# Two fused transformer blocks on one core: all modulation columns as row products on VectorE

## The chip, the cores and the metric

The kernel runs on one core of a Trainium2 chip. The metric is the device time of one execution in microseconds (us), lower is better. TensorE (PE) multiplies, VectorE (DVE) and ScalarE (ACT) work elementwise, GpSimd (POOL) and SyncE (SP) issue transfers here.

## The reference

Two blocks run one after the other on 256 tokens of width 1024, each with two layers. Every layer of both blocks is modulated: a conditioning vector goes through silu and is multiplied by a matrix, and the result, cut into columns of 1024, shifts, scales and gates the token stream.

```python
# first block, per layer l (6 columns of 1024 = 48 units of 128)
mod = silu(c) @ ada_w[l] + ada_b[l]
x = x + g1 * mixer(modulate(rms_norm(x), sh1, sc1))
x = x + g2 * peer_ffn(modulate(rms_norm(x), sh2, sc2), w_query, sub_keys, expert_u, expert_v)
# second block, per layer i (9 columns of 1024 = 72 units of 128)
m  = silu(c_2) @ ada_w_2[i] + ada_b_2[i]
mc = silu(c_ctx_2) @ ada_w_2[i] + ada_b_2[i]     # context: only layer 0, first 5 columns are read
```

`peer_ffn` picks 16 experts for each of 8 heads and token out of 128 x 128. The kernel computes all experts densely: a first phase (`expert_u`, 128 units) makes the activations of all experts, a second (`expert_v`, 128 units) sums them with gates.

## The kernel before, in words

**Stream.** All weights are one stream of units of 128 x 1024 float32 (512 KB). SP loads them in a written order into a ring of four slots, `raw`; the load of unit q waits until unit q-4 is released (`load`, line 496). A weight unit is split into a high and a low part: ACT copies each half to `wh` (`hi`, line 635, L643), DVE writes raw minus `wh` to `wl` (`lo`, line 1096, L1101), and PE makes three products of each 128 x 128 piece (L1906 to L1908), 24 matmuls in a unit. `wh` and `wl` hold two units.

**Stages.** `plan` (line 110) writes the order: for each layer of the first block `w_in`, `attn_o`, `w_out`, `query`, `sub_keys`, `expert_u`, `expert_v`; then the second block `ffn.0.0`, its context copy `ffn.0.0.x`, `kv_ctx`, `qkv`, `na_o`, `ffn.0.1`, `ffn.1.0`, `conv_in`, `conv_o`, `ffn.1.1`. DVE, ACT and PE each walk through that order by hand written code. In `w_out` DVE adds the product to the stream (L1157) and ACT squares it (L874). `pairs` (line 1161) runs the feed-forward stages in 22 rounds of three units, with hooks of vector work after chosen rounds.

**Modulation, two ways.** (1) *Folded on DVE.* `fold` (line 1106, L1119) multiplies a unit of the weights, laid out as columns, by the silu of the vector, which stands in every partition, and sums along the row: one column of 128 values. The unit takes a slot of the ring and is folded right behind `lo` of the unit before it. `folds_after` (line 73) says where: 16 at the start, 32 in layer 0 up to `query.0`, and 104 of the second block's in `ffn.0.0`, `ffn.0.0.x`, `kv_ctx`, `qkv`, `ffn.0.1` and `ffn.1.0`. (2) *On PE.* The 48 units of the first block's layer 1 (`ada1.1`) and 40 units of the second block's layer 0 (`ada2.0`, for both vectors) go through PE in the experts' first phase, after units with u % 5 in (0, 2), up to u = 119 in layer 0 and u = 99 in layer 1 (`MIXED_U`, line 58). `ada_unit` (line 2066, L2072) makes four matmuls with a moving block of 256; each eight units a block is copied by ACT (`copy_block`, line 790), turned by PE (`turn_block`, line 2056) and placed by ACT (`place_block`, line 796).

**The experts' first phase.** For u up to 59, DVE picks the experts (routing: maxima, replaced and found values over the scores), with `feed()` (line 1460), which is `lo` of the next unit, at chosen places between. From u = 60 (`GATES_FROM`) there is one batch of four tokens a unit: DVE makes two one-hot tiles (L1592, L1594), ACT weights one (L915), PE multiplies them (`spread_choices`, line 2193, L2200), ACT copies the result (L925). Each unit ends with ACT's gelu (L921) and POOL's store of it (L597). `add_bias` (line 1258) adds the bias to modulation columns before they are used.

Of the kernel before, what the change touches and what calls it, by code (L numbers as in the profile page):

```python
# [29 lines left out]
P = 128  # L30
# [26 lines left out]
MIXED_ADA = ("ada1.1", "ada2.0")  # L57
MIXED_U = (120, 100)
# [14 lines left out]
def folds_after():  # L73


    out = {}

    def put(stage, units, name, columns):
        assert len(units) == len(columns), (stage, len(units), len(columns))
        for k, column in zip(units, columns):  # L80
            out[stage, k] = (name, column)

    def rows_of(js):

# [7 lines left out]
    two = list(range(FOLDED_2))  # L92
# [9 lines left out]
FOLDED_2 = 72 - 40 + 72  # L102


def fold_column(n):

    return (0, 40 + n) if n < 32 else (1, n - 32)


def plan():  # L110
# [18 lines left out]
    for l in range(DEPTH):  # L129
# [7 lines left out]
        add(MIXED_ADA[l], 2 * MIXED_U[l] // 5, False)  # L137
# [15 lines left out]
    for name, units in (("fold1", 48), ("fold2", FOLDED_2)):  # L153
        fold_at[name] = placed
        placed += units

    order = [("fold1", k) for k in range(FIRST_FOLDS)]
    starts = {}
    for name, units, split, source, groups in rows:
        if name in MIXED_ADA:  # L160
            continue
        starts[name] = len(order)
        for k in range(units):
            order.append((name, k))
# [21 lines left out]
COLUMNS = [("c", KT), ("c_2", KT), ("c_ctx", KT), ("final_norm", KT)]  # L186
# [66 lines left out]
def build(nc, ctx, stream, columns, tables, x_in, ctx_in, rpb, c_rows, h_spill, out):  # L253
# [31 lines left out]
    c_first = side[:, 0:D].rearrange("p (n w) -> p n w", w=D // 2)  # L285
    c_second = side[:, :].rearrange("p (n w) -> p n w", w=6 * T)[:, :, 4 * T:6 * T]
# [13 lines left out]
    cs = sb("cs", [P, 3, KT])  # L300
    mod1 = sb("mod1", [P, DEPTH, 48])
    mod2 = sb("mod2", [P, DEPTH, 72, 2])
    mod2_flat = mod2[:, :, :, :].rearrange("p l n c -> p (l n c)")
# [5 lines left out]
    rows = sb("rows", [P, 2 * KT * P // 4])  # L309

    GROUPS, GROUP = 4, 32
    vectors = sb("vectors", [P, KT, GROUP])
    BLOCK = KT * P // GROUPS
# [55 lines left out]
    SUMS = 30720  # L369
    token_sums = tiles(SUMS, TT, D)  # L370
# [18 lines left out]
    silu_ready = sem("silu_ready")  # L389
    c_loaded = [sem(f"c_loaded{i}") for i in range(2)]  # L390
    c_ready = sem("c_ready")
    folded = sem("folded")
    block_copied = sem("block_copied")
    block_turned = sem("block_turned")
    block_placed = sem("block_placed")
# [67 lines left out]
    BLOCKS = [stages[name].units // KT for name in MIXED_ADA]  # L463

    def after(l, u):

        return [2 * (u // 5) + u % 5 // 2] if u < MIXED_U[l] and u % 5 in (0, 2) else []
# [17 lines left out]
    def _(sp):  # L485
        seen = Seen()

        def released(q):

            name, k = order[q]  # L490
            if name in fold_at:
                return folded, folded_units.index((name, k)) + 1
# [11 lines left out]
        sp.dma_start(c_first, c_rows[0, :, :].rearrange("p (n w) -> p n w", w=D // 2)).then_inc(c_loaded[0], 16)  # L504
# [30 lines left out]
        for st in stages.values():  # L535

            if st.name in MIXED_ADA:
                continue
            if st.name.startswith("expert_u") or st.name in mixed_stages:
# [35 lines left out]
    def _(pool):  # L575

        pool.dma_start(X[:, :, :], x_in).then_inc(x_loaded, 16)
# [6 lines left out]
        pool.memset(vectors[:, :, :], 0.0).then_inc(constants_set, 1)  # L584
        pool.wait_ge(constants_set, 4)
# [20 lines left out]
        pool.dma_start(c_second, c_rows[1, :, :].rearrange("p (n w) -> p n w", w=D // 2)).then_inc(c_loaded[1], 16)  # L606
# [23 lines left out]
    def _(act):  # L630
# [143 lines left out]
        def silu_of_rows(view, n):  # L774

            act.wait_ge(c_loaded[n], 16)
            act.activation(view, view, ACT.Silu).then_inc(c_ready, 1)

        silu_of_rows(c_first, 0)
        act.wait_ge(prepared, 48)  # L780
        act.wait_ge(constants_set, 5)
        for k, name in enumerate(("c", "c_2", "c_ctx")):
            last = act.activation(cs[:, k, :], column(name, 0, KT), ACT.Silu)
        last.then_inc(act_step, steps.one())
        act.wait_ge(act_step, steps.n)
        act.activation(vectors[:, :, 0], cs[:, 1, :], ACT.Copy)
        act.activation(vectors[:, :, 1], cs[:, 2, :], ACT.Copy)
        act.activation(vectors[:, :, 2], cs[:, 0, :], ACT.Copy).then_inc(silu_ready, 1)

        def copy_block(n, used):  # L790

            act.wait_ge(raw_used, used)
            act.activation(rows[:, (n % 2) * BLOCK:(n % 2 + 1) * BLOCK], banks[6 + n % 2][:, 0:BLOCK],
                           ACT.Copy).then_inc(block_copied, 1)

        def place_block(n, nv, dst):

            row = 0 if nv == 2 else 2
            act.wait_ge(block_turned, n + 1)
            turned = banks[2 + n % 2][:, 0:2 * P].rearrange("p (f g r) -> p g f r", f=2, g=GROUPS)  # L800
            act.activation(dst.rearrange("p (g f v) -> p g f v", f=2, v=nv), turned[:, :, :, row:row + nv],
                           ACT.Copy).then_inc(block_placed, 1)

        def block_home(n):

            if n < 6:
                return 1, mod1[:, 1, KT * n:KT * (n + 1)]
            return 2, mod2_flat[:, 2 * KT * (n - 6):2 * KT * (n - 5)]
# [4 lines left out]
        for l in range(DEPTH):  # L813
# [87 lines left out]
            first, first_block = l * BATCHES, BLOCKS[0] * l  # L901
            used = stages[MIXED_ADA[l]].r
            for u in range(KEYS):
# [5 lines left out]
                b = u - GATES_FROM  # L909
                if 0 <= b < BATCHES:  # L910
# [11 lines left out]
                b = u - GATES_FROM - 2  # L922
# [1620 lines left out]
```

## Time and profile before

| | us |
|---|---|
| median of 3 runs | 3757.21 |
| lowest and highest | 3756.78, 3763.63 |
| the profiled execution, its own time | 3760.27 |
| its span in the trace | 3758.1 |
| PE busy | 3591.4 (96%) |
| DVE busy | 2690.9 (72%) |
| ACT busy | 2034.6 (54%) |
| bytes moved | 784.65 MB, mean 209 GB/s |

Busy shares are averages over stages. A PE matmul's end is modelled, so the pace of units, read from one ACT instruction to the same one of the next unit, says more than the share. "Released by" in a wait names what came last by the profile.

### The profile page before, as it was taken

What the parts mean: (1) busy time and instruction counts of PE and PEld (TensorE: products, weight loads), DVE (VectorE), ACT (ScalarE), POOL (GpSimd) and SP (SyncE); (2) the same over time, 40 slices, a digit from 0 to 9 for tenths busy, and PEclk for the clock granted to TensorE, in tenths of its full rate; (3) what the DMA queues carried; (4) which work ended last, traced back from release to release, by engine and by line L of the source; (5) the groups of instructions that cost most, each with busy time, mean ns of one, the idle gap of its engine ahead of it and who ended that gap; (6) DMA issues with size and microseconds to landing.
All of it is one profiled execution on the core that took longest, in us unless ns stands there. A gap on an engine that the chain in (4) does not pass through costs nothing.

```text
span 3758.1 us, 71030 instructions
## 1 busy us (share of the span) xinstructions
PE 3591.4 (96%) x24950; PEld 3281.8 (87%) x24950; DVE 2690.9 (72%) x5336; ACT 2034.6 (54%) x4235; POOL 217.2 (6%) x335
## 2 busy tenths in 40 slices
PE   5989999999999989999999998999998899999898
PEld 5889999998888889999998887899987689898898
DVE  6774986667777664896667777777777577776765
ACT  4544447775555554447775555544444454545444
POOL 0000111110000000111110001010001010100000
PEclk8999999999999999999999999999999999999999
DMA  8456776667775434776647778776765167575453
GB/s 281 154 187 213 269 269 213 213 220 240 242 241 190 137 129 168 249 264 230 214 170 254 242 240 252 229 246 214 245 219 168 32 201 248 197 247 167 140 185 133
DMA packets 245507, 784.65 MB, mean 209 GB/s; under 512 B 30048, under 2 KB 62816, under 8 KB 245040
## 3 DMA queue, kind: packets, MB, share of 16 engines
q1 hardware_dynamic: 230544, 737.78, 59.5%
q0 software_dynamic: 14752, 44.12, 3.3%
q8 instruction: 125, 2.05, 0.2%
q14 instruction: 86, 0.70, 0.1%
HBM read 747.17 MB, written 34.60 MB: 208 GB/s over the span
## 4 chain that ended last, share of the span: by engine, by line
PE 77%; DVE 7%; PEld 6%; issue 3%; DMA 3%; ACT 2%; PEldq 1%; SPq 0%; ACTq 0%; POOL 0%; DVEq 0%
PE bank L1906 17%; PE bank L1907 17%; PE bank L1908 17%; PE bank L1979 5%; PE bank L1980 5%; PE bank L1981 5%; PE bank L2200 3%; PEld bank L1979 2%; PEld bank L1980 2%; PEld bank L1981 2%; DVE wl L1101 2%; DMA raw<-stream 2%; PE bank L2050 2%; PE bank L2072 1%; ACT wh L643 1%
## 5 line engine op out<-in xcount | busy, mean ns | idle before, releaser
L1101 DVE TENSOR_TENSOR wl<-raw,wh 128x512 fp32r<-128x512 f32 x2180 | 1453.8, 690 | 687.2 <-ACT wh L643 684.8
L643 ACT ACTIVATE wh<-raw 128x512 fp32r<-128x512 f32 x2180 | 1316.5, 629 | 825.3 <-PE bank L1981 427.0
L1906 PE MATMUL bank<-XH,wh 128*128 128x256 f32 x5184 | 1504.0, 290 | 88.0 <-DVE XL L1226 49.9
L1907 PE MATMUL bank<-XL,wh 128*128 128x256 f32 x5184 | 1477.4, 285 | 0.0
L1908 PE MATMUL bank<-XH,wl 128*128 128x256 f32 x5184 | 1476.6, 285 | 0.0
L1906 PEld LDWEIGHTS bank<-XH,wh 128*128 128x128 f32 x5184 | 1004.4, 194 | 129.6 <-issue 92.0
L1907 PEld LDWEIGHTS bank<-XL,wh 128*128 128x128 f32 x5184 | 1005.9, 194 | 4.0 <-issue 1.0
L1908 PEld LDWEIGHTS bank<-XH,wl 128*128 128x128 f32 x5184 | 1004.7, 194 | 0.0
L1979 PE MATMUL bank<-wh,AH 128*128 128x512 f32 x1464 | 571.4, 390 | 1.4 <-DVE AL L1609 1.0
L1980 PE MATMUL bank<-wl,AH 128*128 128x512 f32 x1464 | 570.8, 390 | 0.0
L1981 PE MATMUL bank<-wh,AL 128*128 128x512 f32 x1464 | 569.6, 389 | 0.0
L1981 PEld LDWEIGHTS bank<-wh,AL 128*128 128x128 f32 x1464 | 274.9, 188 | 58.0
L1979 PEld LDWEIGHTS bank<-wh,AH 128*128 128x128 f32 x1464 | 275.3, 188 | 57.3 <-DVE wl L1101 1.7
L1980 PEld LDWEIGHTS bank<-wl,AH 128*128 128x128 f32 x1464 | 275.3, 188 | 52.8
L921 ACT ACTIVATE side<-bank 128x256 f32<-128x256 f32 x256 | 98.3, 384 | 323.6 <-PE bank L1908 319.6
L686 ACT ACTIVATE arena<-bank 128x256 f32<-128x256 f32 (+1 forms) x208 | 79.2, 383 | 319.4 <-PE bank L1908 319.3
L597 POOL DMA_DIRECT2D h_spill<-side x256 | 138.4, 541 | 1491.1 <-ACT side L921 1478.5
L1594 DVE TENSOR_TENSOR side<-iota,routed 128x512 f32<-128x512 f32 x128 | 88.7, 693 | 152.9 <-PE bank L2200 152.9
L1119 DVE SCALAR_TENSOR_TENSOR raw<-raw,side 128x1024 f32<-128x1024 f32 x152 | 186.2, 1225 | 15.0 <-DMA raw<-stream 14.8
L1906 PE MATMUL bank<-X2H,wh 128*128 128x256 f32 x544 | 157.0, 289 | 6.2 <-DVE wl L1101 5.9
L915 ACT ACTIVATE side<-side,routed 128x128 f32<-128x128 f32 x512 | 162.9, 397 | 0.0
L1601 DVE TENSOR_TENSOR side<-side,arena 128x256 f32<-128x256 f32 x256 | 159.5, 623 | 0.1
(237 smaller groups left out, 3146.4 us busy)
## 6 DMA issues: line engine op xcount, KB each, us to landing
raw<-stream SPq DMA_DIRECT2D x1340, 512.0 KB, 4.3
h_spill<-side POOLq DMA_DIRECT2D x256, 128.0 KB, 3.7
side<-h_spill SPq DMA_DIRECT2D x256, 128.0 KB, 3.8
arena<-rpb POOLq DMA_DIRECT2D x4, 1024.0 KB, 25.3
arena<-tables POOLq DMA_DIRECT2D x2, 832.0 KB, 9.5
X<-x_t POOLq DMA_DIRECT2D x1, 1024.0 KB, 8.2
side<-ctx_t POOLq DMA_DIRECT2D x8, 128.0 KB, 3.9
arena<-ctx_t POOLq DMA_DIRECT2D x1, 1024.0 KB, 8.3
```

Source lines behind the costliest of these rows:

```text
L597: pool.dma_start(h_spill[u, :, :], HS[:, u % 2, :]).then_inc(h_stored[u % 2], 16)
L643: act.activation(wh[:, n % 4, :], raw[:, q % 4, HALF * half:HALF * (half + 1)], ACT.Copy).then_inc(hi_ready, 1)
L915: last = act.activation(by_weight[:, b % 2, n * P:(n + 1) * P], unweighted[:, n * P:(n + 1) * P], ACT.Copy, scale=routed[:, 2, t:t + 1])
L1101: tt_op(wl[:, n % 4, :], raw[:, q % 4, HALF * half:HALF * (half + 1)], wh[:, n % 4, :].bitcast(F32), SUB).then_inc(lo_ready, 1)
L1119: dve.scalar_tensor_tensor(unit, unit, 1.0, c, MUL, MUL, accum_out=dst).then_inc(folded, 1)
L1601: tt_op(AP_[:, j % 2, :].unsqueeze(2), HV[:, j % 4, :].unsqueeze(2), gates[:, :, bass.ds(j + more, 1)], MUL).then_inc(gate_done, 1)
L1906: pe.matmul(out, wh[:, n % 4, a:b], moving_h, start=start, stop=False, skip_group_check=check)
L1907: pe.matmul(out, wh[:, n % 4, a:b], moving_l, start=False, stop=False, skip_group_check=check)
L1908: return pe.matmul(out, wl[:, n % 4, a:b], moving_h, start=False, stop=stop, skip_group_check=check)
L1979: pe.matmul(out, high, wh[:, n % 4, :], start=first, stop=False)
L1980: pe.matmul(out, high, wl[:, n % 4, :], start=False, stop=False)
L1981: last = pe.matmul(out, low, wh[:, n % 4, :], start=False, stop=final)
```

## The change

The PE way is taken out, with its copies, turns and placements on ACT and PE and the small ACT work that made the vectors for it. All 48 + 48 + 144 units are folded on DVE; the 40 units of the second block's layer 0 that the context reads too are folded twice, once with each vector (280 folded products, 152 before). The number of units streamed, 240, is the same. Where they go:

```diff
-    put("w_in.0", (2, 3, 4, 6, 7, 8, 10, 11, 12, 14, 16, 18, 20, 22, 24, 26), "fold1", one[16:32])
-    put("attn_o.0", (1, 3, 5, 7), "fold1", one[32:36])
-    put("w_out.0", (1, 2, 4, 5), "fold1", one[36:40])
-    put("query.0", range(2, 32, 4), "fold1", one[40:48])
...
-    put("ffn.0.0", rows_of(range(2, 21)), "fold2", two[0:19])
-    put("ffn.0.0.x", rows_of(range(21)), "fold2", two[19:40])
-    put("kv_ctx", (0, 1, 2, 3, 5, 7, 9, 11, 13, 15), "fold2", two[40:50])
-    put("qkv", range(1, 24, 2), "fold2", two[50:62])
-    put("ffn.0.1", rows_of(range(21)), "fold2", two[62:83])
-    put("ffn.1.0", rows_of(range(21)), "fold2", two[83:104])
+    def beside_layer(l, name, columns):
+
+        put(f"w_in.{l}", (2, 3, 4, 6, 7, 8, 10, 11, 12, 14, 16, 18, 20, 22, 24, 26), name, columns[0:16])
+        put(f"attn_o.{l}", (1, 3, 5, 7), name, columns[16:20])
+        put(f"w_out.{l}", (1, 2, 4, 5), name, columns[20:24])
+        put(f"query.{l}", range(2, 32, 4), name, columns[24:32])
...
+    beside_layer(0, "fold1.0", one[16:48])
+    put("expert_u.0", range(66, 114, 3), "fold1.1", one[0:16])
+    beside_layer(1, "fold1.1", one[16:48])
+    two = list(range(DEPTH * 72))
+    put("query.1", range(0, 32, 4), "fold2", two[40:48])
+    put("expert_u.1", range(66, 114, 3), "fold2", two[0:16])
+    put("ffn.0.0", rows_of(range(2, 21)), "fold2", two[16:35])
+    put("ffn.0.0.x", rows_of(range(21)), "fold2", two[35:40] + two[48:64])
+    put("kv_ctx", (0, 1, 2, 3, 5, 7, 9, 11, 13, 15), "fold2", two[64:74])
+    put("qkv", (0, 1, 2, 3, 5, 7, 9, 11, 13, 15, 17, 19, 21, 23), "fold2", two[74:88])
+    put("ffn.0.1", rows_of(range(21)), "fold2", two[88:109])
+    put("ffn.1.0", rows_of(range(21)), "fold2", two[109:130])
+    put("conv_in", range(1, 13, 2), "fold2", two[130:136])
+    put("ffn.1.1", rows_of(range(8)), "fold2", two[136:144])
```

The fold itself, with the second product ahead of the first where n < 40:

```diff
             unit = raw[:, q % 4, :].rearrange("p (n w) -> p n w", w=D // 2)
+            if name == "fold2" and n < 40:
+                dve.wait_ge(context_c_loaded, 16)
+                dve.scalar_tensor_tensor(unread, unit, 1.0, c_kept[:, :, :], MUL, MUL,
+                                         accum_out=second_mod(0, n, n + 1, 1))
             dve.scalar_tensor_tensor(unit, unit, 1.0, c, MUL, MUL, accum_out=dst).then_inc(folded, 1)
```

The silu of all three vectors' rows is made at the start: the first vector's stays in SBUF (`c_kept`), the other two (1 MB together) are loaded at the head of POOL's queue, go through ACT, and are stored to a DRAM scratch. They come back in 512 KB loads on POOL's queue: two copies of the second vector's once the operands of `w_in.1` are made, ahead of layer 1's table load, which used to be issued as soon as layer 0's second phase ended; the context vector's into `c_kept` after layer 1's last column; and one in the place where the rows of `c_2` were loaded before.

```diff
+        for n in range(2):
+            pool.dma_start(c_rows_at[:, n * D:(n + 1) * D], c_rows[1 + n, :, :]).then_inc(rows_loaded, 16)
         pool.dma_start(X[:, :, :], x_in).then_inc(x_loaded, 16)
...
             if l:
+                pool.wait_ge(xl_ready, made["w_in.1"])
+                pool.dma_start(c_query, c_spill[0, :, :].rearrange("p (n w) -> p n w", w=D // 2))\
+                    .then_inc(query_c_loaded, 16)
+                pool.dma_start(c_experts, c_spill[0, :, :].rearrange("p (n w) -> p n w", w=D // 2))\
+                    .then_inc(experts_c_loaded, 16)
                 pool.wait_ge(space_free, l)
...
+            if l == 0:
+                pool.wait_ge(c_ready, 2)
+                for n in range(2):
+                    pool.dma_start(c_spill[n, :, :], c_rows_at[:, n * D:(n + 1) * D]).then_inc(c_stored, 16)
+                pool.wait_ge(c_stored, 32)
+            else:
+                pool.wait_ge(folded, folds_by("fold1.1", 47))
+                pool.dma_start(c_kept[:, :, :], c_spill[1, :, :].rearrange("p (n w) -> p n w", w=D // 2))\
+                    .then_inc(context_c_loaded, 16)
```

The batches of the gates keep their pace, one a unit from u = 60 on. `add_bias` waits for the last column it needs and runs in smaller pieces (layer 1 of the first block as layer 0; the second block's just ahead of each use). Stages that hold folds are written out on SP, ACT and DVE where they were loops.

## Rows read from the trace of the kernel before

**Rows 1.** the page, part 1: busy us, share of the span, instructions

```profile
PE 3591.4 (96%) x24950; PEld 3281.8 (87%) x24950; DVE 2690.9 (72%) x5336; ACT 2034.6 (54%) x4235; POOL 217.2 (6%) x335
```

**Rows 2.** windows: us, then PE, PEld, DVE, ACT, POOL busy, clock, DMA share, GB/s

```profile
371.00:556.00 185.00, 183.40 (x1558) 169.64 (x1557) 171.43 (x524) 88.92 (x181) 30.81 (x57) 1.00 0.78 270
1891.00:1973.00 82.00, 82.00 (x699) 82.00 (x698) 53.16 (x83) 64.39 (x167) 11.35 (x21) 1.00 0.49 167
```

**Rows 3.** source line L2072, the modulation products on PE

```profile
L2072 PE MATMUL bank<-raw,vectors x704: 379/391/404, 371.0 to 1866.2; 128*32 128x256 f32 x176
```

**Rows 4.** timeline, ACT, layer 0 routing: start us, us, engine, line

```profile
429.42 0.38 ACT L921 ACTIVATE side<-bank 128x256 f32<-128x256 f32 x1 [2.21 <-PE bank L1908]
...
432.30 0.38 ACT L921 ACTIVATE side<-bank 128x256 f32<-128x256 f32 x1 [1.18 <-PE bank L1908]
```

**Rows 5.** timeline, ACT, layer 0 gates

```profile
646.79 0.38 ACT L921 ACTIVATE side<-bank 128x256 f32<-128x256 f32 x1 [0.69 <-PE bank L1908]
...
651.49 0.38 ACT L921 ACTIVATE side<-bank 128x256 f32<-128x256 f32 x1 [1.53 <-PE bank L1908]
...
655.25 0.38 ACT L921 ACTIVATE side<-bank 128x256 f32<-128x256 f32 x1 [0.50 <-PE bank L1908]
...
659.78 0.38 ACT L921 ACTIVATE side<-bank 128x256 f32<-128x256 f32 x1 [1.39 <-PE bank L1908]
```

**Rows 6.** timeline, DVE, layer 1 gates

```profile
1902.40 1.29 DVE L1101 TENSOR_TENSOR wl<-raw,wh 128x512 fp32r<-128x512 f32 x2
1904.00 0.69 DVE L1592 TENSOR_TENSOR side<-iota,routed 128x512 f32<-128x512 f32 x1 [0.31 <-ACT side L915]
```

**Rows 7.** timeline, ACT, layer 1 gates

```profile
1906.46 1.27 ACT L915 ACTIVATE side<-side,routed 128x128 f32<-128x128 f32 x4
1908.43 0.38 ACT L921 ACTIVATE side<-bank 128x256 f32<-128x256 f32 x1 [0.70 <-PE bank L1908]
```

**Rows 8.** the page, part 5: the folded products

```profile
L1119 DVE SCALAR_TENSOR_TENSOR raw<-raw,side 128x1024 f32<-128x1024 f32 x152 | 186.2, 1225 | 15.0 <-DMA raw<-stream 14.8
```

**Rows 9.** chain that ended last, in order of time: start us, us, what

```profile
38.76 1.68 DVE arena L1248
...
214.42 2.20 DVE arena L1429
...
250.79 3.47 PE bank L2050 x16
...
353.65 14.56 PE bank L2183 x128
...
1192.20 1.76 DVE arena L1248
...
1366.66 2.20 DVE arena L1429
...
1399.02 3.47 PE bank L2050 x16
...
1502.97 14.56 PE bank L2183 x128
...
2554.99 2.65 DVE arena L1675 x8
```

**Rows 10.** windows of the start

```profile
5.00:10.00 5.00, 0.00 (x0) 0.00 (x0) 1.49 (x3) 0.46 (x1) 0.00 (x0) 1.00 1.01 417
30.00:38.00 8.00, 0.00 (x0) 0.00 (x0) 6.04 (x12) 2.30 (x4) 0.00 (x0) 0.50 0.94 312
```

**Rows 11.** timeline, DVE, ffn.0.0, rounds 6 and 11

```profile
2415.90 0.41 DVE L1685 TENSOR_TENSOR side<-side,bank 128x256 f32<-128x256 f32 x1
...
2425.10 0.41 DVE L1685 TENSOR_TENSOR side<-side,bank 128x256 f32<-128x256 f32 x1
...
2460.24 0.41 DVE L1685 TENSOR_TENSOR side<-side,bank 128x256 f32<-128x256 f32 x1
...
2468.74 0.41 DVE L1685 TENSOR_TENSOR side<-side,bank 128x256 f32<-128x256 f32 x1
```

More of the change, by code:

```diff
@@ L152, in plan @@
     fold_at = {}
-    for name, units in (("fold1", 48), ("fold2", FOLDED_2)):
+    for name, units in (("fold1.0", 48), ("fold1.1", 48), ("fold2", 72 * DEPTH)):
         fold_at[name] = placed
         placed += units
-    order = [("fold1", k) for k in range(FIRST_FOLDS)]
+    order = [("fold1.0", k) for k in range(FIRST_FOLDS)]
     starts = {}
     for name, units, split, source, groups in rows:
-        if name in MIXED_ADA:
-            continue
         starts[name] = len(order)
@@ L307, in build @@
     routed = sb("routed", [P, 3, T])
[L309 to L313, printed above, removed]
+    c_kept = sb("c_kept", [P, 2, D // 2])
     small = sb("small", [P, 64])
@@ L369, in build @@
     SUMS = 30720
+    c_experts = tiles(SUMS + D, 2, D // 2)
+    unread_experts, unread_ffn = tiles(SUMS, 2, D // 2), tiles(QT, 2, D // 2)
     token_sums = tiles(SUMS, TT, D)
@@ L388, in build @@
     constants_set = sem("constants_set")
[L389 to L390 removed]
+    c_loaded = sem("c_loaded")
+    rows_loaded = sem("rows_loaded")
+    c_stored = sem("c_stored")
+    query_c_loaded = sem("query_c_loaded")
+    experts_c_loaded = sem("experts_c_loaded")
+    context_c_loaded = sem("context_c_loaded")
+    ffn_c_loaded = sem("ffn_c_loaded")
     c_ready = sem("c_ready")
     folded = sem("folded")
[L393 to L395 removed]
     mod_ready = sem("mod_ready")
@@ L460, in build, with folds_by, batches_of @@
     block = ctx.enter_context(nc.Block())
-    BLOCKS = [stages[name].units // KT for name in MIXED_ADA]
-    def after(l, u):
-        return [2 * (u // 5) + u % 5 // 2] if u < MIXED_U[l] and u % 5 in (0, 2) else []
+    def folds_by(name, k):
+        return folded_units.index((name, k)) + 1
+    def batches_of(u):
+        return [b for b in range(BATCHES) if GATES_FROM + b == u]
     CTX_FROM = 103
@@ L772, in copy_sum @@
                                ACT.Copy).then_inc(sum_copied[0], 1)
[L774 to L779, printed above, removed]
+        act.wait_ge(c_loaded, 16)
+        act.activation(c_kept[:, :, :], c_kept[:, :, :], ACT.Silu).then_inc(c_ready, 1)
+        act.wait_ge(rows_loaded, 32)
+        act.activation(c_rows_at, c_rows_at, ACT.Silu).then_inc(c_ready, 1)
         act.wait_ge(prepared, 48)
[L781 to L808, printed above, removed]
+        act.wait_ge(constants_set, 4)
         rms = A(RMS, T)
@@ L899, in row_highs @@
                 act.activation(AH[:, j % 2, :], AP_[:, j % 2, :], ACT.Copy).then_inc(row_high, 1)
-            first, first_block = l * BATCHES, BLOCKS[0] * l
-            used = stages[MIXED_ADA[l]].r
+            first = l * BATCHES
             for u in range(KEYS):
@@ L1266, in add_bias @@
             else:
-                bias = column(f"ada_b_2.{l}", a, b - a)
-                view = mod2[:, l, a:b, 0:sides]
-                step(tt_op(view, view, bias.unsqueeze(2).broadcast_to([P, b - a, sides]), ADD))
+                for side in range(sides):
+                    view = second_mod(l, a, b, side)
+                    step(tt_op(view, view, column(f"ada_b_2.{l}", a, b - a), ADD))
             settle()
@@ L1317, in _ @@
                 for n in range(FIRST_FOLDS):
-                    fold("fold1", n)
+                    fold("start", "fold1.0", n)
                 dve.wait_ge(prepared, 48)
-                add_bias(0, 1, 0, 16, units=FIRST_FOLDS)
+                add_bias(0, 1, 0, 16)
                 scale_plus_one(scale[:, :], mod1[:, l, 8:16], column(f"norm_mix.{l}", 0, KT))
@@ L1458, in _ @@
             fed = [1]
+            dve.wait_ge(c_stored, 32)
             def feed():
@@ L1588, in _ @@
             for b in range(BATCHES):
-                feed()
+                while fed[0] <= GATES_FROM + b:
+                    feed()
                 if b or l:
@@ L1811, in _ @@
         dve.wait_ge(view_ready, 1 + 2 * KT)
-        add_bias(0, 2, 40, 72, units=48 + 32)
+        add_bias(0, 2, 40, 48)
+        add_bias(0, 2, 48, 72)
         residual_factor(0, 24, 0, 1.0)
@@ L2208, in _ @@
                     pe.wait_ge(route_evacuated, 8 * (l + 1))
-                for a in after(l, u):
-                    ada_unit(first_block + a // KT, a % KT, place[MIXED_ADA[l], a])
-                n = block_after(l, u, 3)
-                if n is not None:
-                    turn_block(first_block + n)
                 if u == TURN_AT:
```

169 lines of the change are left out of this document (59 added, 110 removed).

## The prediction

> **What bounds the kernel now.** I read the busy shares first [rows 1]: PE is busy 96% of the span, DVE 72%. An average over stages says little, so the windows come next. The change takes its work off PE in one place only, the experts' first phase, so that is where any gain must come from. It has two parts with different limits. In the routing part of layer 0 (units 0 to 57) PE is busy 183.4 of 185 us, but DVE is busy 171.4 of the same 185 [rows 2]: PE leads by little, and DVE idles only 13.6 us. In the gates part (from unit 60) PE is busy all of 82 us, DVE 53.2 and ACT 64.4 [rows 2]. There PE bounds alone.
>
> Then the work to be removed [rows 3]: 704 matmul records, 8 for each of 88 units. Their own durations overlap and say nothing of their price; the pace of units does. ACT's gelu of one unit to that of the next is 2.88 us in the routing part where no modulation unit stands between [rows 4]. In the gates part it is 3.76 us without one, 4.53 with one, and 4.70 with one and the turn of a block [rows 5]. So a modulation unit costs 0.77 us of PE, a block's turn 0.17.
>
> **Gates part.** It holds 24 of layer 0's 48 modulation units and 16 of layer 1's 40: 40 x 0.77 = 30.8, and 7 turns x 0.17 = 1.2, together 32.0 us, all on the path. What comes instead is 16 folds in layer 0 and 16 double folds in layer 1, one every third unit, on DVE. A fold is one instruction of 1.225 us [rows 8], and its accumulator read hides in the pitch. After `lo` DVE is free at 1903.69; it makes the one-hot at 1904.00 to 1904.69, and ACT takes it up only at 1906.46 [rows 6, 7]: 1.77 us of slack. A double fold of 2.45 brings that one-hot to 1906.83, 0.4 late; ACT's weighting would be late by that, but ACT then waits 0.70 for PE before the gelu [rows 7], which takes it in. A single fold is not late at all. I take 0 for both; if the cover is gone, the next thing late is the gelu, then PE's bank. Bounds: 0 and 16 x 1.225 + 16 x 2.45 = 58.8.
>
> **Routing part.** 24 units x 0.77 and 2 turns x 0.17, 18.8 us of PE, go in each layer, and nothing is added. DVE's work stays, 171.4 of 185, so 13.6 is the most that can come back. It can't all come: where DVE has little to do between two `feed()` PE's 2.88 stays the limit, and DVE idles still. I take half, 7 us a layer, 14 in both; bounds 0 and 27.
>
> **Start.** DVE's 16 folds wait for their loads. The transfers run at 417 GB/s early and 312 late with the engines' share near 1 [rows 10]: the start is bound by transfers. The change adds 1.05 MB of reads at the head of POOL's queue, ahead of X, and 1.05 MB of writes. 2.1 MB take 5.0 us at 417 and 6.7 at 312. Some hides behind DVE, which catches up a little (its folds are 16 x 1.225 = 19.6 of the 38.8 us up to the reciprocal, [rows 9]): I take 4.5, bounds 0 and 6.7. ACT's larger silu and the removed small ones lie in its idle time.
>
> The page "DMA: Bandwidth & Descriptors" of the Trainium skill, section Specifications, gives a core about 358 GB/s of HBM as its limit; the row of 417 GB/s is above it, so the row decides here. By the page's figure the 2.1 MB would be an estimated 5.9 us and the sum 1.4 us higher.
>
> **Layer 1 from `w_in.1` to `query.1`.** It gets the 32 folds that layer 0 has, at the same units, and layer 0 against layer 1 in the trace is that experiment. From the reciprocal to `sub_keys`: 353.65 - 38.76 = 314.9 in layer 0, 1502.97 - 1192.20 = 310.8 in layer 1, a difference of 4.1. Nearly all is in `w_out`: 36.4 (214.42 to 250.79) against 32.4 (1366.66 to 1399.02) [rows 9]. There each fold stands between `lo` and DVE's residual, for which ACT's square and then ACT's next copy wait, so 4 folds cost about 1 us each; elsewhere DVE has idle time. So +4.1. The 8 further folds of `query.1` I take at 0 by the same comparison (its 8 folds of layer 0 did not show), bounds 0 and 9.8. The bias additions become more and smaller: +0.5.
>
> **POOL's queue in layer 1.** The table load is now issued behind the wait for the operands of `w_in.1` and behind two loads of 512 KB, while the ring runs 1.5 units a product unit. Together 1.9 MB, 4.5 us of all transfer engines at 417 GB/s. The ring is four units ahead, and the tables are needed only after 12 units of 2.88, 35 us: I take +1.5, bounds 0 and 4.5. The context vector's load stands ahead of the first store of layer 1 and lands during `sub_keys`: 0.
>
> **ffn.0.0 and after.** 19 folds become double. A plain round takes 8.50 us and is PE's; a round with operand work hooked on takes 9.20 [rows 11], because DVE and ACT hand tiles to one another there. In that chain a fold is exposed in full. Five rounds (5 to 9) have it: 5 x 1.225 = 6.1; the rest hides. In `ffn.0.0.x` five more, of which one stands right ahead of centring the context, which is on the chain (at 2554.99) [rows 9], 1.2, and 0.4 for two more bias additions. In `qkv` two more folds beside the bias mask's additions, worth at most 2.4: I take 1.0. The folds of `conv_in` and `ffn.1.1` are 0: plain rounds have room. Bounds for all this: 2 and 20.
>
> **Sum.** Gains 32.0 + 14 = 46.0. Costs 4.5 + 4.1 + 0.5 + 1.5 + 6.1 + 1.6 + 1.0 = 19.3. Net 26.7 us off the profiled execution's own 3760.3: 3733.6. The median of the three runs is 3.1 lower, so the forecast is 3757.2 - 26.7 = 3730.5, say 3731.
>
> **Rivals.**
> (A) *The routing part gives nothing, and the transfers cost their upper bounds.* DVE's 171 of 185 us and hand-written places of `feed()` speak for it, PE's 99% busy against. +14 + 2.2 + 3.0: 3750.
> (B) *DVE's room in routing is used in full and the start hides its bytes.* For it, POOL's loads are early; against, the start's full transfer engines. -13 - 4.5: 3713.
> (C) *Slower: the gates' folds are exposed.* Place: the chain one-hot, weighting, `spread_choices`, where a double fold is 0.4 over the slack of 1.77 and only ACT's 0.70 covers it. If the batches can't catch up within three units, each fold is paid: up to 58.8, 3790. It decides from 46% of that, 27 us; below, the change still gains. Against it: DVE is idle 28.8 of 82 us there [rows 2], 1.3 us in each unit of 3.76.
> (D) *Double folds in `ffn.0.0` are exposed in most rounds, not five.* 14 more rounds x 1.225 = 17: 3748.
> That the modulation doesn't leave PE can't be: L2072 is gone from the code.
>
> **How the numbers follow.** Forecast 0.58, A 0.12, B 0.12, C 0.05, D 0.13. The range 3713 to 3751 holds all but C and the outer ends. A measurement of this kernel tells about 0.2%, 7.5 us, from no change: same is 3749.7 to 3764.7. The forecast, B, and most of D and half of A are below: faster 0.87. Same 0.08, slower 0.05.
>
> **What would show it.** In the profile after: no L2072; gelu to gelu 3.76 through the gates of both layers, also at units with a fold; routing near 178 us to unit 57, with DVE hardly idle; the first reciprocal (L1248) near 43 us in place of 38.76; `w_out` of layer 1 as long as layer 0's 36.4; rounds 5 to 9 of `ffn.0.0` near 10.4 us. Rounds of the gates above 3.9 us would mean C; a start or a `w_in.1` longer by over 7 us would mean that transfers cost more than I took.

## The result, and the profile after

The changed kernel takes 3729.35 us (median of 4 runs, 3724.82 to 3734.11), the kernel before beside it on the same chip 3760.42 (3756.78 to 3764.11): a ratio of 0.9916, 95% interval 0.9902 to 0.9930. The forecast was 3731 us, in a range of 3713 to 3751. Measured again, five times, it took 3730.32 against 3758.65, ratio 0.9921 (0.9908 to 0.9935). The profiled execution of the changed kernel, 3734.11 by its own time with a span of 3732.3, is the slowest of its four, so what follows explains 26.2 us (3760.27 - 3734.11); the medians say 31.1 and, the second time, 28.3.

The page, parts 1 and 5, against [rows 1, 8]; L1092 is the last product of a fold, L1090 the product with the context vector:

```profile
PE 3533.5 (95%) x24224; PEld 3265.2 (87%) x24224; DVE 2830.1 (76%) x5602; ACT 2021.7 (54%) x4202; POOL 227.7 (6%) x341
...
L1092 DVE SCALAR_TENSOR_TENSOR raw<-raw,side 128x1024 f32<-128x1024 f32 x128 | 156.8, 1225 | 0.2 <-DMA raw<-stream 0.2
```

PE lost 57.9 us of busy time, and the span 25.8: more than half of what PE was relieved of didn't reach the end. DVE gained 139.2. (A bracket in the rows below holds the engine's idle time before the instruction, and what ended it.) The windows, against [rows 2], first the whole routing part of layer 0 (units 0 to 57), then 82 us of layer 1's gates with folds in them:

```profile
375.00:552.00 177.00, 169.30 (x1371) 165.49 (x1371) 170.59 (x524) 86.87 (x177) 30.81 (x57) 1.00 0.69 215
1860.00:1942.00 82.00, 81.92 (x690) 81.55 (x689) 57.27 (x96) 63.02 (x161) 11.89 (x22) 1.00 0.61 198
```

Routing: PE is no longer full, it idles 7.7 of 177 us, and DVE idles 6.4 (13.6 of 185 before). Gates: PE is as full as before. The timeline there, ACT, with the gelu (L897), the weighting (L891) and the copy of the gates (L902), against [rows 5, 7]:

```profile
1874.61 0.38 ACT L897 ACTIVATE side<-bank 128x256 f32<-128x256 f32 x1 [0.69 <-PE bank L1884]
...
1878.38 0.38 ACT L897 ACTIVATE side<-bank 128x256 f32<-128x256 f32 x1 [0.70 <-PE bank L1884]
...
1880.33 1.28 ACT L891 ACTIVATE side<-side,routed 128x128 f32<-128x128 f32 x4
1882.15 0.38 ACT L897 ACTIVATE side<-bank 128x256 f32<-128x256 f32 x1 [0.53 <-PE bank L1884]
```

and DVE in the same stretch, against [rows 6]:

```profile
1876.12 1.28 DVE L1068 TENSOR_TENSOR wl<-raw,wh 128x512 fp32r<-128x512 f32 x2
1877.32 1.22 DVE L1090 SCALAR_TENSOR_TENSOR arena<-raw,c_kept 128x1024 f32<-128x1024 f32 x1
...
1878.46 1.22 DVE L1092 SCALAR_TENSOR_TENSOR raw<-raw,arena 128x1024 f32<-128x1024 f32 x1
...
1879.61 0.69 DVE L1563 TENSOR_TENSOR side<-iota,routed 128x512 f32<-128x512 f32 x1
1880.82 1.28 DVE L1068 TENSOR_TENSOR wl<-raw,wh 128x512 fp32r<-128x512 f32 x2
1883.65 1.28 DVE L1068 TENSOR_TENSOR wl<-raw,wh 128x512 fp32r<-128x512 f32 x2
1887.42 1.28 DVE L1068 TENSOR_TENSOR wl<-raw,wh 128x512 fp32r<-128x512 f32 x2
```

Gelu to gelu is 3.77 us on both sides of a double fold. The one-hot behind it starts at 1879.61, 1.9 us later than one pace behind the one before (1873.95); ACT's weighting is 0.15 late, and the gelu not at all. Last the chain in order of time, against [rows 9]. Two rows have the source lines 1221 (the first reciprocal of a norm) and 1400 (the start of `w_out`); `bank L2026` is the mean of the squares that ends a stage; `ACT arena L803` comes late in `w_in` (the last units of the stage stand behind it):

```profile
42.51 1.67 DVE arena L1221
...
218.56 2.20 DVE arena L1400
...
254.94 3.47 PE bank L2026 x16
...
1168.37 1.76 DVE arena L1221
1180.32 7.45 DMA raw<-stream
1214.11 2.34 ACT arena L803
...
1347.03 2.20 DVE arena L1400
...
1383.42 3.47 PE bank L2026 x16
...
2348.42 3.46 PE bank L2026 x16
...
2515.67 3.46 PE bank L2026 x16
```

Stage by stage, both from their profiled executions (the same instruction to the same instruction; layer 0, layer 1):

| stretch | before | after | difference |
|---|---|---|---|
| up to the first reciprocal | 38.8 | 42.5 | +3.8 |
| `w_in` of layer 1, from the reciprocal to the row of L803 | 41.8 | 45.7 | +3.9 |
| `w_out` | 36.4, 32.4 | 36.4, 36.4 | 0, +4.0 |
| routing, gelu of unit 0 to 57 | 185.0, 185.4 | 176.8, 176.8 | -8.2, -8.6 |
| gelu of unit 57 to 60 | 10.0, 10.0 | 9.3, 9.3 | -0.7, -0.7 |
| gates, gelu of unit 60 to 127 | 269.3, 263.3 | 250.2, 250.6 | -19.1, -12.7 |
| `expert_v.1` and up to `ffn.0.0` | 405.4 | 406.7 | +1.3 |
| `ffn.0.0` | 161.4 | 167.3 | +5.8 |
| `ffn.0.0.x` | 203.3 | 204.7 | +1.4 |
| `kv_ctx` to the end of `na_o` | 241.6 | 244.9 | +3.3 |
| the four stages after it | 729.0 | 728.8 | -0.1 |

### The profile page after: what moved, and what is told of

The parts are those of the page before. It is cut to its first block, busy times and chain, and to the rows that moved or that the text cites. A ratio compares the mean times of both kernels' runs of the same rounds, so it can differ in the third digit from the quotient of the medians.

```text
span 3732.3 us, 68910 instructions
## 1 busy us (share of the span) xinstructions
PE 3533.5 (95%) x24224; PEld 3265.2 (87%) x24224; DVE 2830.1 (76%) x5602; ACT 2021.7 (54%) x4202; POOL 227.7 (6%) x341
## 4 chain that ended last, share of the span: by engine, by line
PE 69%; DVE 15%; PEld 7%; issue 3%; ACT 3%; DMA 2%; PEldq 1%; SPq 0%; ACTq 0%; DVEq 0%; POOL 0%
PE bank L1882 15%; PE bank L1884 15%; PE bank L1883 15%; PE bank L1955 5%; PE bank L1956 5%; PE bank L1957 5%; DVE wl L1068 5%; PE bank L2154 3%; PEld bank L1957 2%; PEld bank L1955 2%; PEld bank L1956 2%; DMA raw<-stream 2%; PE bank L2026 2%; ACT wh L650 1%; DVE raw L1092 1%
## 5 line engine op out<-in xcount | busy, mean ns | idle before, releaser
L1957 PEld LDWEIGHTS bank<-wh,AL 128*128 128x128 f32 x1464 | 275.0, 188 | 57.9
L693 ACT ACTIVATE arena<-bank 128x256 f32<-128x256 f32 x208 | 79.0, 382 | 327.6 <-PE bank L1884 327.3
L897 ACT ACTIVATE side<-bank 128x256 f32<-128x256 f32 x256 | 98.1, 383 | 288.1 <-PE bank L1884 284.3
L891 ACT ACTIVATE side<-side,routed 128x128 f32<-128x128 f32 x512 | 162.8, 396 | 0.7
L1092 DVE SCALAR_TENSOR_TENSOR raw<-raw,side 128x1024 f32<-128x1024 f32 x128 | 156.8, 1225 | 0.2 <-DMA raw<-stream 0.2
L1884 PE MATMUL bank<-X2H,wl 128*128 128x256 f32 x544 | 155.4, 286 | 0.0
```

Of the source, the lines that this page charges most:

```text
L891: last = act.activation(by_weight[:, b % 2, n * P:(n + 1) * P], unweighted[:, n * P:(n + 1) * P], ACT.Copy, scale=routed[:, 2, t:t + 1])
L1092: dve.scalar_tensor_tensor(unit, unit, 1.0, c, MUL, MUL, accum_out=dst).then_inc(folded, 1)
L1884: return pe.matmul(out, wl[:, n % 4, a:b], moving_h, start=False, stop=stop, skip_group_check=check)
L1957: last = pe.matmul(out, low, wh[:, n % 4, :], start=False, stop=final)
```

## The experiments

Each is the changed kernel with one edit, or, where it says so, the kernel before. Experiments 1 to 9 have one time each; the kernel before took 3763.33 beside 1 to 4, and 3765.26 beside 5 to 8. Experiments 1 to 4 ran on one chip, 5 to 8 on another, 9 and 10 on a third. Times of stretches are from their traces, against the table above. One stretch differs from trace to trace even where no edit touches it: up to the first reciprocal the changed kernel takes 42.5 us in its first trace, and 42.8 to 43.6 in the seven others that leave the start as it is. So a stretch is compared with those of the same chip where the difference is small.

**1. The rows of the two vectors later.** Their loads, silu and stores move from the head of the queues to behind `w_in.0`; ACT makes the silu in four pieces between products.

```diff
-        for n in range(2):
-            pool.dma_start(c_rows_at[:, n * D:(n + 1) * D], c_rows[1 + n, :, :]).then_inc(rows_loaded, 16)
...
             if l == 0:
-                pool.wait_ge(c_ready, 2)
+                pool.wait_ge(group_free, 2 + stages["w_in.0"].g + W_IN_TILES)
+                for n in range(2):
+                    pool.dma_start(c_rows_at[:, n * D:(n + 1) * D], c_rows[1 + n, :, :]).then_inc(rows_loaded, 16)
+                pool.wait_ge(c_ready, 5)
```

> The rows of the two vectors are loaded, put through silu (in four pieces, on ACT between units of attn_o.0) and spilled after w_in.0, not at the start. Theory (the start is bound by transfers, and 2.1 MB more of them cost 3.75 us): the first reciprocal of DVE comes back from 42.51 us to 38.8 (within 0.7), attn_o.0 grows by 0 to 1.5 us, the span falls by 2 to 4 us. Rival (the first reciprocal is late because DVE's folds or the new semaphores are slower): it stays near 42.5.

**2. The same bytes, other order.** The two loads only go behind those of X, the columns and the first tables on POOL's queue.

```diff
-        for n in range(2):
-            pool.dma_start(c_rows_at[:, n * D:(n + 1) * D], c_rows[1 + n, :, :]).then_inc(rows_loaded, 16)
         pool.dma_start(X[:, :, :], x_in).then_inc(x_loaded, 16)
...
         pool.dma_start(iota[:, :], tables[:, tab_at["iota"][0]:tab_at["iota"][0] + P]).then_inc(prepared, 16)
+        for n in range(2):
+            pool.dma_start(c_rows_at[:, n * D:(n + 1) * D], c_rows[1 + n, :, :]).then_inc(rows_loaded, 16)
```

> Only the order on POOL's queue is changed: X, the columns and the small tables first, the two row loads behind them. Theory (bytes, whatever their order): the first reciprocal stays at 42.5 us within 1 us. Rival (order: X and the columns come late, so the squares, the root and the bias are late): it comes back to 39 to 40 us.

Measured: 3728.38 and 3728.52 us. The reciprocal, in the chains of the first and the second:

```profile
38.38 1.67 DVE arena L1235
```

```profile
41.96 1.68 DVE arena L1221
```

Moving the bytes away gives 4.1 us of the start back (42.51 to 38.38), moving them behind X only 0.55. Against experiments 3 and 4, on the same chip, whose first reciprocals start at 43.38 and 43.30, it is about 5 and 1.4. So it is mostly the bytes that the start pays for; the place of X in the queue may be a quarter of it. The first pays 0.6 back in the stretch behind `w_in.0`, up to `w_out` (126.3 from 125.7).

**3. Layer 1's loads later.** The tables are loaded first, as in the kernel before; the two copies of the second vector's silu come after `w_in.1`.

```diff
             if l:
-                pool.wait_ge(xl_ready, made["w_in.1"])
-                pool.dma_start(c_query, c_spill[0, :, :].rearrange("p (n w) -> p n w", w=D // 2))\
-                    .then_inc(query_c_loaded, 16)
-                pool.dma_start(c_experts, c_spill[0, :, :].rearrange("p (n w) -> p n w", w=D // 2))\
-                    .then_inc(experts_c_loaded, 16)
                 pool.wait_ge(space_free, l)
...
             else:
+                pool.wait_ge(group_free, 2 + stages["w_in.1"].g + W_IN_TILES)
+                pool.dma_start(c_query, c_spill[0, :, :].rearrange("p (n w) -> p n w", w=D // 2))\
+                    .then_inc(query_c_loaded, 16)
+                pool.dma_start(c_experts, c_spill[0, :, :].rearrange("p (n w) -> p n w", w=D // 2))\
+                    .then_inc(experts_c_loaded, 16)
                 pool.wait_ge(folded, folds_by("fold1.1", 47))
```

> Layer 1's table load is issued at the end of layer 0's second phase again, and the two copies of the second vector are loaded only after w_in.1, while attention runs. Theory (the 1.9 MB beside a ring at 1.75 units a product unit starve the first units of w_in.1): from the reciprocal to the head sums 52.95 us falls to the 50.3 of layer 0, which has the same folds; the span falls by 2.5 us. Rival (the folds themselves cost it): it stays at 52.9.

Measured: 3730.23 us; `w_in.1` falls from 45.7 to 41.6 (1168.32 to 1209.94, chain), by more than I expected. Windows of the same 20 us, 12 us behind a reciprocal that starts at 1168.3 to 1168.4 in both, of the changed kernel and of this one; then POOL's issues in the changed kernel:

```profile
1180.00:1200.00 20.00, 16.78 (x127) 16.57 (x128) 12.39 (x21) 7.53 (x17) 0.00 (x0) 0.91 0.85 307
```

```profile
1180.00:1200.00 20.00, 19.47 (x162) 19.26 (x162) 14.98 (x26) 9.62 (x20) 0.00 (x0) 1.00 0.85 298
```

```profile
1177.42 0.54 POOL L585 DMA_DIRECT2D side<-c_spill  x1 [364.58 <-DVE XL L1199]
1177.95 0.54 POOL L587 DMA_DIRECT2D arena<-c_spill  x1
1178.48 0.53 POOL L590 DMA_DIRECT2D arena<-tables  x1
```

The three loads, 1.9 MB, share the transfer engines with the ring just when DVE folds three units in four. Without them PE has 162 matmul records in the 20 us, with them 127, and idles 3.2 us, and its granted clock falls to a mean of 0.91. The transfer engines' share is 0.85 in both: they aren't short of time in the mean, the ring's loads come late (one stands for 7.45 us in the chain above, and for 5.29 in this one). `w_in.1` has its 16 folds in both kernels of this comparison: the loads cost all of its 4 us, the folds nothing. The time as a whole moved by less than single runs differ, so the verdict rests on the stretch.

**4. A third product in every double fold of `expert_u.1`**, to find how much cover the gates have.

```diff
                 dve.scalar_tensor_tensor(unread, unit, 1.0, c_kept[:, :, :], MUL, MUL,
                                          accum_out=second_mod(0, n, n + 1, 1))
+                if host == "expert_u.1":
+                    dve.scalar_tensor_tensor(tiles(SUMS - D, 2, D // 2), unit, 1.0, c_kept[:, :, :], MUL, MUL,
+                                             accum_out=small[:, 63:64])
```

> In the gates part of layer 1 each double fold has a third product beside it (its result is not used), 16 x 1.225 = 19.6 us of DVE work more. Theory (the cover is 1.77 us of slack at the one-hot plus 0.70 us of ACT's wait for PE, 2.47 in all, and a double fold of 2.45 just fits): three products of 3.68 are 1.2 us over it, so units with a fold take up to 4.9 us in place of 3.77, 10 to 19 us in all. Rival (DVE runs ahead and the cover spans several units, 28.8 of 82 us idle): the pace stays 3.77 and the span within 2 us.

Measured: 3732.9 us; gates of layer 1 250.7 us, from 250.6. My expectation was wrong; the rival is right on the sum. DVE around the same unit as above, and ACT's weighting in it:

```profile
1875.95 1.28 DVE L1068 TENSOR_TENSOR wl<-raw,wh 128x512 fp32r<-128x512 f32 x2
...
1881.31 1.28 ACT L891 ACTIVATE side<-side,routed 128x128 f32<-128x128 f32 x4 [1.19 <-DVE side L1566]
...
1881.80 1.28 DVE L1068 TENSOR_TENSOR wl<-raw,wh 128x512 fp32r<-128x512 f32 x2
1884.21 1.28 DVE L1068 TENSOR_TENSOR wl<-raw,wh 128x512 fp32r<-128x512 f32 x2
1887.27 1.28 DVE L1068 TENSOR_TENSOR wl<-raw,wh 128x512 fp32r<-128x512 f32 x2
1891.04 1.28 DVE L1068 TENSOR_TENSOR wl<-raw,wh 128x512 fp32r<-128x512 f32 x2
```

`lo` starts 5.85, 2.41, 3.06 and 3.77 us apart; with two products it was 4.70, 2.83 and 3.77. DVE is late by 2.1 and makes it good over the next two units, because it needn't wait there. The lateness does get as far as ACT: its weighting waits 1.19 us for DVE, and the gelu of each such unit comes after 4.28 us, the next one after 3.27. PE doesn't feel it: it is busy 81.91 of 82 us (1860 to 1942), as with two products. So 3.67 us of products in one place cost nothing in the sum, though the waits of a single unit, 1.77 and 0.70, don't add up to that.

**5. `qkv` with 12 folds as before**, two moved to `kv_ctx`.

```diff
-    put("kv_ctx", (0, 1, 2, 3, 5, 7, 9, 11, 13, 15), "fold2", two[64:74])
-    put("qkv", (0, 1, 2, 3, 5, 7, 9, 11, 13, 15, 17, 19, 21, 23), "fold2", two[74:88])
+    put("kv_ctx", (0, 1, 2, 3, 4, 5, 6, 7, 9, 11, 13, 15), "fold2", two[64:76])
+    put("qkv", range(1, 24, 2), "fold2", two[76:88])
```

> qkv has its 12 folds of before again (after units 1, 3, 5, ...), and the two others go to kv_ctx, after units 4 and 6. Theory (folds beside the bias mask's additions in the first units of qkv are exposed, and those in kv_ctx's idle time are not): from the mean of kv_ctx (2720.2 us) to that after na_o (2985.5 us), 265.3 us, comes back to 262 to 263; the span falls by 2 to 3 us. Rival (the longer stage comes from the many small bias additions, or is chance): it stays at 265.

Measured: 3732.1 us, `kv_ctx` to `na_o` 244.3, from 244.9 (and from 245.1 in the three others on the same chip). My theory fell: the two folds are worth 0.8 at most of the 3.3. The same stretch in the second profile of the unaltered changed kernel is 242.6, and between 242.7 and 245.1 in the eight other variants; the kernel before has 241.6, and 240.1 in the variant of experiment 9. In the first profile the chain has a wait for the ring here that most of the others lack:

```profile
2771.05 5.70 DMA raw<-stream
```

The stretch is longer by 3.3 in the first two profiles (244.9 against 241.6), and by 2.5 in two that ran on one chip (242.6 against 240.1): about 2.5 to 3.3 us of it are real. What causes them stays open. It is hardly the ring alone: ACT's copies wait 6.5 us for loads there in the first profile and not at all in the kernel before, but in this experiment they wait only 0.2, and the stretch is 244.3.

**6. No folds in rounds 5 to 9 of `ffn.0.0`.** 20 double folds stand in `expert_u.1` in place of 16, one more in `kv_ctx`.

```diff
-    put("expert_u.1", range(66, 114, 3), "fold2", two[0:16])
-    put("ffn.0.0", rows_of(range(2, 21)), "fold2", two[16:35])
+    put("expert_u.1", range(62, 122, 3), "fold2", two[0:20])
+    put("ffn.0.0", rows_of([2, 3, 4] + list(range(10, 21))), "fold2", two[20:34])
```

> Rounds 5 to 9 of ffn.0.0 hold no fold; four more double folds stand in expert_u.1 (20, after every third unit from 62) and one fold more in kv_ctx. Theory (in these rounds DVE and ACT hand tiles to one another and a double fold is exposed twice 1.225): rounds of 9.5 to 10.26 us fall to 8.5, or to 8.7 where hooked work remains, so ffn.0.0 is shorter by 6 to 8 us, and expert_u.1 keeps its pace of 3.77. Rival (the hooked work alone makes the rounds long): they stay over 9 us, and the stage falls by under 3 us.

Measured: 3723.31 us. `ffn.0.0` takes 158.9, from 167.3, a little more than I expected, and the gates of layer 1 keep their 250.6. DVE's product that ends a round (L1656) in the changed kernel, against [rows 11], and in this one:

```profile
2402.32 0.41 DVE L1656 TENSOR_TENSOR side<-side,bank 128x256 f32<-128x256 f32 x1
...
2412.58 0.41 DVE L1656 TENSOR_TENSOR side<-side,bank 128x256 f32<-128x256 f32 x1
...
2420.99 0.41 DVE L1656 TENSOR_TENSOR side<-side,bank 128x256 f32<-128x256 f32 x1
```

```profile
2390.87 0.41 DVE L1656 TENSOR_TENSOR side<-side,bank 128x256 f32<-128x256 f32 x1
2399.37 0.41 DVE L1656 TENSOR_TENSOR side<-side,bank 128x256 f32<-128x256 f32 x1
```

Rounds of 10.26 become 8.50. So the fold was exposed there, as predicted, and one fold had cost even the kernel before: 158.9 is 2.5 below its 161.4. The 9.20 of [rows 11] was not the operand work's alone, as the prediction has it: with that work and no fold a round takes 8.50. `ffn.0.0.x` pays 1.1 back.

**7. `w_out` without folds**, its four moved into `w_in`, which then has 20, the last four behind units 28 to 31.

```diff
-        put(f"w_in.{l}", (2, 3, 4, 6, 7, 8, 10, 11, 12, 14, 16, 18, 20, 22, 24, 26), name, columns[0:16])
-        put(f"attn_o.{l}", (1, 3, 5, 7), name, columns[16:20])
-        put(f"w_out.{l}", (1, 2, 4, 5), name, columns[20:24])
+        put(f"w_in.{l}", (2, 3, 5, 6, 8, 9, 11, 12, 14, 15, 16, 18, 20, 22, 24, 26, 28, 29, 30, 31), name, columns[0:20])
+        put(f"attn_o.{l}", (1, 3, 5, 7), name, columns[20:24])
```

> The four folds of w_out in both layers go to w_in, which has 20 in place of 16, spaced wider at its start and to its last unit. Theory (in w_out a fold lies on the chain lo, residual, square, copy; in w_in it is covered): w_out falls from 36.3 us to 32.4 in both layers, w_in keeps its length within 1 us in each, the span falls by 7 to 8 us. Rival (the transfers of w_in can't carry more): w_in grows by 2 us or more in each layer and takes back half of it or more.

Measured: 3730.51 us. `w_out` is 32.4 in both layers (1348.41 to 1380.84 in layer 1's chain), 3.9 less, and `w_in` up to the row of L803 is no longer. But the stretch from 7 us behind that row to `w_out` is 127.5 and 127.7, from 125.7. The first 50 us behind the row are as before; then, where the chain of the changed kernel is PE's alone, that of this one waits for two loads of the ring, around the folds of units 28 to 31:

```profile
1275.56 5.00 DMA raw<-stream
...
1283.71 4.87 DMA raw<-stream
```

So half of the gain comes back, as the rival said, only later than it said; by this chain it is loads of the ring that come late where four units in a row have a fold behind them. The term of `w_out` is confirmed, the new place was badly chosen.

**8. Less of DVE in routing.** The second of the two key look-ups is left out: the column index is a copy of the row index. So 13.7 us of DVE's instructions a layer are left out.

```diff
                 for side, top, dst in ((0, TOPA, RI), (1, TOPB, RJ)):
+                    if side:
+                        feed()
+                        feed()
+                        settle()
+                        step(dve.tensor_copy(A(RJ, P), A(RI, P)))
+                        feed()
+                        continue
```

> The kernel after the change, with one of the two look-ups of the routing (compare, multiply and sum of 2048 elements, 3 x 2.28 us, for each half of the tokens) left out and the other's result copied, so the second key index is not computed; 13.7 us of DVE work less in each layer. Theory (DVE bounds the routing part now, at 167 of 170 us busy, except where PE's 2.88 us does): the 176.8 us to unit 57 fall by 4 to 9 us in each layer. Rival (PE or the waits between engines bound it): under 1.5 us.

Measured: 3728.96 us, routing 174.8 in each layer, from 176.8. The window of layer 0's routing:

```profile
375.00:552.00 177.00, 170.32 (x1394) 167.73 (x1393) 159.21 (x523) 87.65 (x179) 31.35 (x58) 1.00 0.69 218
```

and the gelus of the changed kernel, then of this one, at the place of the look-up:

```profile
445.54 0.38 ACT L897 ACTIVATE side<-bank 128x256 f32<-128x256 f32 x1 [1.74 <-PE bank L1884]
448.92 0.38 ACT L897 ACTIVATE side<-bank 128x256 f32<-128x256 f32 x1 [1.96 <-PE bank L1884]
452.34 0.38 ACT L897 ACTIVATE side<-bank 128x256 f32<-128x256 f32 x1 [2.00 <-PE bank L1884]
```

```profile
444.64 0.38 ACT L897 ACTIVATE side<-bank 128x256 f32<-128x256 f32 x1 [1.74 <-PE bank L1891]
448.04 0.38 ACT L897 ACTIVATE side<-bank 128x256 f32<-128x256 f32 x1 [1.98 <-PE bank L1891]
450.92 0.38 ACT L897 ACTIVATE side<-bank 128x256 f32<-128x256 f32 x1 [1.46 <-PE bank L1891]
```

Of 13.7 us less work, 2.0 reach the pace, between theory and rival: the rounds of the look-up fall from 3.42 and 3.41 to PE's 2.88, and the other long rounds (3.29, 3.62, 3.52, 4.24, 4.36) stay. DVE now idles 17.8 of 177 us, and the time is as good as the same. DVE's total doesn't set routing; in the look-up's rounds it is the work between two `feed()`. Not all long rounds need be DVE's: in that of 4.36, which the next makes up in part (2.18), the chain passes through a table load of 1.28 us that ACT makes for its exponential (L906, at 456.15).

**9. The same cut in the kernel before.**

> The kernel before with the second key look-up of each layer's routing left out (its index row is copied from the first's), the edit that took 2.0 us of 176.8 off the changed kernel's routing part. Theory (before, PE bound the routing part: 183.4 of 185 us busy; only in the changed kernel do DVE's chunks between two feeds show): units 0 to 57 fall by 0.5 us or less in each layer, and the time by under 1 us. Rival (the long rounds were DVE's before as well, in the same measure): they fall by 2 us in each layer, 4 us in all.

Measured: 3758.32 us beside 3758.65 for the kernel before. Its routing is 186.5 and 187.1 us, 1.5 and 1.7 longer than in the trace of the kernel before: neither expectation. At the look-up itself the theory holds: before, 3.41, 3.63, 3.17, and now 3.41, 3.64, 2.88, so 0.3 in that place, where the changed kernel had 1.06. The longer rounds stand elsewhere, the first of them behind unit 1 (3.84 and, in layer 1, 4.43, where it was 2.88), ahead of everything that was cut. There ACT's copy of the next unit waits 2.40 and 2.99 us for a load of the ring, against 1.09 and 0.30 before. Why the load is late stays open.

**10. What paid, together.** The edits of 1, 3 and 6, and of 7 with the folds closer from unit 14 on and none behind unit 28; `qkv` has 12 folds and `kv_ctx` 13.

```diff
-        put(f"w_in.{l}", (2, 3, 4, 6, 7, 8, 10, 11, 12, 14, 16, 18, 20, 22, 24, 26), name, columns[0:16])
+        put(f"w_in.{l}", (2, 3, 5, 6, 8, 9, 11, 12, 14, 15, 16, 18, 19, 20, 22, 23, 24, 26, 27, 28), name, columns[0:20])
...
+    put("kv_ctx", (0, 1, 2, 3, 4, 5, 6, 7, 8, 9, 11, 13, 15), "fold2", two[63:76])
+    put("qkv", range(1, 24, 2), "fold2", two[76:88])
```

> The four parts that paid when each was tried alone, together: the two rows' loads, silu and spill behind w_in.0 (start -3.7 us, the stretch after w_in.0 +0.6), the loads of layer 1 behind its tables and after w_in.1 (w_in.1 -4.0), no folds in rounds 5 to 9 of ffn.0.0 and 20 double folds in expert_u.1 (ffn.0.0 -8.3, ffn.0.0.x +1.2), and the folds of w_out moved into w_in, now 20 of 32 units with none behind unit 28 (w_out -3.9 in each layer; the stretch after w_in, which paid 1.8 back when folds stood at units 29 to 31, near 0). Theory (these costs lie in series on the path, and add up): -3.7 + 0.6 - 4.0 - 8.3 + 1.2 - 7.8 = -22.0 against the changed kernel, 3707; with the 1.8 still paid twice, 3711. Rival (the folds packed closer into w_in and kv_ctx outrun the ring of four loads, or DVE, so that a good part comes back there): w_in longer by 2 us or more in each layer and kv_ctx by 2, 3713 to 3718. Below 3700 or above 3720 neither holds.

> The changed kernel itself, for a comparison on the same chip in the same rounds. Expected: 3729, within 4 us of its median so far, and 0.991 of the kernel before.

Measured: 3706.43 us (median of 4 runs, 3706.05 to 3706.69), 0.9859 of the kernel before (0.9844 to 0.9874), and 3730.32 for the changed kernel again (0.9921). It beats both, by 23.9 and 52.2. Its chain:

```profile
38.73 1.67 DVE arena L1234
214.25 2.20 DVE arena L1413
...
246.67 3.47 PE bank L2039 x16
...
1160.75 1.76 DVE arena L1234
1201.85 2.34 ACT arena L801
...
1335.84 2.20 DVE arena L1413
1368.54 3.47 PE bank L2039 x16
```

Start 38.7, `w_in.1` 41.1 (1160.75 to 1201.85), `w_out` 32.4 and 32.7, `ffn.0.0` 159.0. The stretches behind the row of L803 are 126.3 and 126.8. Layer 0's 0.6 is what experiment 1 paid there; layer 1's 1.1 is more than half of experiment 7's 1.8, and its chain again waits 4.98 us for a load of the ring (at 1261.67). `ffn.0.0.x` is 2.7 longer, where 1.2 were expected, and no run shows why. In sum the costs lay in series, as the theory said (3707 expected); up to the row of L803 `w_in` is no longer, and `kv_ctx` to `na_o` is 242.7, beside 242.6, so the rival fell.

## Why the prediction was right, and where not

- **Gates: 32.0 forecast, 31.8 found** (269.3 + 263.3 - 250.2 - 250.6); the three units from 57 to 60, which the prediction had left out, gave another 1.4. The price of 0.77 a unit, from one pace against another, holds to under 1% where the 320 records of these 40 units, at their own 391 ns [rows 3], would have said 125 us. That the cover holds was right. Its working was too tight: it set 2.45 against 1.77 + 0.70, and experiment 4 laid 3.67 there at no cost. Rival C was further off than its 0.05 says.
- **Routing: 14 forecast, 16.8 found.** Half of DVE's room hit near, and that was luck, for it is no rule: experiment 8 gave DVE 13.7 us more room and 2.0 came back. The bound of 27 from DVE's total held as a ceiling, but it says nothing of where in it the gain comes to lie, for A and B neither. The right reading is the list of paces. At PE's 2.88 nothing more is to be had: 57 rounds of it are 164.2 of the 176.8 us, and 12.6 are the excess of the long rounds. Of that, experiment 8 shows 2.0 to be DVE's; the rest no run took apart. The sign of DVE hardly idle is half true, 6.4 of 177.
- **Start: 4.5 forecast, 3.8 found** in the first profiles, and 5.4 between the second of the changed kernel (43.6) and that of experiment 9 (38.2), which ran on one chip. Experiments 1 and 2 show that it is mostly bytes; rival B, which had them hidden, fell. The window of 5 to 10 us shows 416 GB/s again, so the row was right to decide. The 358 GB/s that the Trainium skill gives ("DMA: Bandwidth & Descriptors", Specifications) are for both cores of a pair streaming, by the same page's section Bandwidth, and one core runs here. The prediction's "1.4 us higher" compares the page's estimate of 5.9 with a term from which something hidden was already taken; like for like, with the 5.0 at 417 GB/s, it is 0.9.
- **Layer 1 as layer 0: 4.1 forecast, 4.0 found in `w_out`**, shown by experiments 7 and 10. The 8 further folds of `query.1` don't show, nor do the 0.5 of the bias additions: in layer 1 the reciprocal of `query` to the gelu of unit 0 takes 117.4 us, from 117.3, and the row of L803 to `w_out` 132.8, from 132.6.
- **POOL's queue: 1.5 forecast, 3.9 found.** This is the term that was mis-sized, by 2.4, inside its bounds of 0 and 4.5. The prediction counted on a ring that is four units ahead. Experiment 3 shows that the loads cost it and the folds alone don't; that the folds, behind three units in four there, had used up the ring's lead is my reading, and no run had the loads without them.
- **`ffn.0.0`: 6.1 forecast, 5.8 found**, with three rounds at 10.26 and two at 9.46 and 9.57, 1.05 to 1.15 longer each than before, where the prediction had five near 10.4. Experiment 6 shows that the folds are exposed there, and that a single one had cost before as well, which the prediction had put down to the operand work. Rival D fell: the plain rounds hid their double folds.
- **`ffn.0.0.x`: 1.6 forecast, 1.4 found. `kv_ctx` to `na_o`: 1.0 forecast, 3.3 found** in the first profiles, 2.5 in the two on one chip. Experiment 5 took the prediction's cause, two more folds in `qkv`, away and got 0.6 to 0.8. So this term's cause was wrong for the most part, and the right one is open.
- The sum, 26.7 forecast and 26.2 found in the profiled executions, is nearer than its terms, and that is luck: the gains in routing and between 57 and 60 were larger by 4.2, POOL's loads and `kv_ctx` dearer by 4.7. The medians differ by 31.1 and 28.3; the profiled execution was the slowest of four, so the table explains 2 to 5 us less than they do. The second profile of the changed kernel is 3.1 us shorter (3729.2), 2.3 of it in `kv_ctx` to `na_o`.

## What to carry to other kernels

Price work on a full engine by the pace of the stage with and without it, never by the sum of its records. In a stage that hands work over at fixed places an engine's idle total is a ceiling and no estimate: look at the longest piece between two hand-overs, and at how many units the consumer is ahead. Work that is cheap in itself costs where it stands in a chain of hand-overs or where its loads meet those of the ring; moving folds by a few units or to another stage, and a few loads by one stage, gave 24 us here, nearly as much as the change itself.

## What the hardware showed that I had not expected

3.67 us of products on DVE in one place, in a pace of 3.77, left no mark on the time: the gelu of that unit came 0.51 us late and the next made it good, while PE stayed busy. And one stretch of one kernel, `kv_ctx` to `na_o`, took 244.9 us in one profile and 242.6 in another, with a wait of 5.70 us for a 512 KB load on the chain of the first.
